# Recurrence chunk stages: the second heads' rounds run four rounds behind the first heads' rounds

## The reference

```python
def step(S, inp):
    w_t, k_t, v_t, a_t, b_t = inp[:5]
    sa = jnp.einsum('bhij,bhj->bhi', S, a_t)
    S = S * w_t[:, :, None, :] + sa[..., None] * b_t[:, :, None, :] + v_t[..., None] * k_t[:, :, None, :]
    y = jnp.einsum('bhij,bhj->bhi', S, inp[5]) if emit else None
    return S, y
...
S, ys = lax.scan(step, state0, xs, reverse=reverse)
```

## Time and profile before

| | us |
|---|---|
| median of 3 executions | 2481.49 (2477.02 to 2490.28) |
| the profiled execution: its time, its span | 2468.01, 2466.2 |
| `rc0`, 906.4 to 951.7 | 45.3 |
| `rc1`, 977.3 to 1023.5 | 46.2 |
| `rl0`, 1173.8 to 1224.7 | 50.9 |
| `rl1`, 1249.8 to 1301.1 | 51.3 |

### The profile page before, as it was taken

The page is one execution under the profiler, slowest core; times in us unless marked ns, Lnnn a source line. Parts: engine busy times, 40 slices in busy tenths (PEclk is TensorE's granted clock), DMA queues, the critical chain, the costliest instruction groups (busy, mean ns, idle before and its releaser), DMA issues. The chain is left out here.

```text
span 2466.2 us, 36848 instructions
## 1 busy us (share of the span) xinstructions
PE 1904.0 (77%) x15507; PEld 1233.3 (50%) x15507; DVE 864.4 (35%) x1268; ACT 637.2 (26%) x986; POOL 200.0 (8%) x279
## 2 busy tenths in 40 slices
PE   5999998668999877797888867667666666666665
PEld 5997996557888766696777752111111101101100
DVE  4654445765455565576564533000000000000000
ACT  3334444344324344333432310000000000000000
POOL 0100001010121043201550000000000000000000
PEclk9999999579999988798996968676766687677676
DMA  5654663016985410051002328999999999999996
GB/s 181 204 186 156 189 195 120 1 68 209 306 277 203 153 40 2 22 174 56 3 3 93 134 109 327 417 417 417 417 418 417 417 417 418 417 418 417 417 417 284
DMA packets 222497, 587.79 MB, mean 238 GB/s; under 512 B 11759, under 2 KB 144334, under 8 KB 189598
## 3 DMA queue, kind: packets, MB, share of 16 engines
q1 hardware_dynamic: 220518, 583.89, 62.8%
q10 hardware_dynamic: 1848, 2.01, 0.2%
HBM read 584.77 MB, written 1.09 MB: 238 GB/s over the span
## 5 line engine op out<-in xcount | busy, mean ns | idle before, releaser
L3056 PE MATMUL ps<-ex_ring,ex_xe 128*32 128x512 f32 x1536 | 282.5, 830 | 150.9 <-DMA ex_ring<-in_exp_w 150.9
L3131 DVE TENSOR_TENSOR ex_hid<-ps,ex_silu 128x512 f32<-128x512 f32 x16 | 11.1, 692 | 890.2 <-PE ps L3056 890.2
L3056 PEld LDWEIGHTS ps<-ex_ring,ex_xe 128*32 128x32 f32 x1536 | 36.7, 124 | 390.7 <-DMA ex_ring<-in_exp_w 368.3
L3077 PE MATMUL ps<-ex_ring,ex_ht 128*32 128x512 f32 x768 | 145.0, 853 | 86.1 <-DMA ex_ring<-in_exp_w 80.5
L209 PE MATMUL ps<-xt_hi,ffn_whi 128*128 128x256 f32 x704 | 205.1, 291 | 7.3 <-DVE xt_lo L372 7.3
L210 PE MATMUL ps<-xt_lo,ffn_whi 128*128 128x256 f32 x704 | 200.9, 285 | 0.0
L211 PE MATMUL ps<-xt_hi,ffn_wlo 128*128 128x256 f32 x704 | 200.6, 285 | 0.0
L181 DVE TENSOR_TENSOR ffn_wlo<-ring,ffn_whi 128x2048 fp32r<-128x2048 f32 x66 | 154.2, 2336 | 108.0 <-ACT ffn_whi L174 107.6
L174 ACT CAST ffn_whi<-ring 128x2048 fp32r<-128x2048 f32 x66 | 125.2, 1901 | 117.4 <-PE ps L211 102.8
L209 PEld LDWEIGHTS ps<-xt_hi,ffn_whi 128*128 128x128 f32 x704 | 136.4, 194 | 17.2 <-issue 17.0
L209 PE MATMUL ps<-mixin_whi,xt_hi 128*128 128x256 f32 (+1 forms) x496 | 137.7, 278 | 3.2 <-DVE xt_lo L372 3.2
(11 more groups left out here) (748 smaller groups left out, 3727.4 us busy)
## 6 DMA issues: line engine op xcount, KB each, us to landing
ex_ring<-in_exp_w SPq DMA_DIRECT2D x288, 1024.0 KB, 24.3
ring<-in_exp_w SPq DMA_DIRECT2D x96, 1024.0 KB, 24.8
ring<-in_w_in SPq DMA_DIRECT2D x55, 1024.0 KB, 5.2
ring<-in_ffn_w_gate SPq DMA_DIRECT2D x22, 1024.0 KB, 6.1
ring<-in_ffn_w_up SPq DMA_DIRECT2D x22, 1024.0 KB, 5.4
ring<-in_ffn_w_down SPq DMA_DIRECT2D x22, 1024.0 KB, 4.9
ffn_mod_tile<-in_mod_w SPq DMA_DIRECT2D x12, 1024.0 KB, 6.3
xn<-in_mod_w SPq DMA_DIRECT2D x12, 1024.0 KB, 6.8
```

The costliest lines, as they stand in the source:

```text
L3056: mm = mm_(ps[32 * q:32 * q + 32, 4 + u, :], xe[:, k], expert_slot(g, n)[:, 512 * q:512 * q + 512], start=k == 0, stop=k == KC - 1)
L3077: mm = mm_(ps[32 * q:32 * q + 32, 7, :], ht[:, k % 4, CAP * f:CAP * f + CAP], w[:, h, 512 * n:512 * n + 512], start=k == 0, stop=k == KC - 1)
L3131: v.tensor_tensor(hid[:], ps[:, 5, :], silu[:], ALU.mult).then_inc(S["hid"], 1)
```

## The change

```diff
-CHUNK_ROUNDS = 10
+CHUNK_ROUNDS, LAG = 10, 4
...
         def order():
-            for it in range(0, len(its), 2):
-                for r in range(CHUNK_ROUNDS):
-                    for j in range(2):
-                        yield its[it + j], r, it + j
+
+            n_steps = CHUNK_ROUNDS * len(its) // 2
+            for step in range(n_steps + LAG):
+                for j in range(2):
+                    k = step - LAG * j
+                    if 0 <= k < n_steps:
+                        it = 2 * (k // CHUNK_ROUNDS) + j
+                        yield its[it], k % CHUNK_ROUNDS, it
...
             if not ctx_only:
                 expand_g2(0)
+            expand(2)
+            if not ctx_only:
                 expand_g2(1)
-            expand(2)
             expand(3)
```

## The result

The changed kernel takes 2581.01 us (median of 4, 2578.94 to 2583.17) against 2485.89 for the kernel before: ratio 1.0385, 95% interval 1.0346 to 1.0424. That is some 95 us slower. The direction was forecast, the size wasn't: 2536 was forecast and 2556 was the upper end of the range.

What follows compares the result with a forecast made beforehand. The stages were taken as bound by each stream's chain of dependent rounds, with nothing beside them to hide growth. Stage growths of 14.9 + 14.5 + 13.7 + 12.8 = 55.9, taken as +55 on 2481.5, gave 2536 us, range 2516 to 2556.

Steps and rivals of the forecast that it cites:

- fronts: Rounds 0 to 3 of a stream's pass; four in a row, 11.6 us each in `rl` stages, replace two shared.
- the sum: Growth of the four chunk stages, 14.9 + 14.5 + 13.7 + 12.8 = 55.9 us, taken as +55.
- the wait for A's round 9: In an `rl` stage, A's second round 0 can't start until A's round 9 is done: 3.9 us.
- the wait for B's: In an `rl` stage, B's round 9 must finish before B's second round 0 starts: 2.1 us.
- The tail: End of an `rl` stage: A's round 9, B's rounds 5 to 9 alone, a wait on ACT; 12.5 us together.
- The costs set at nothing: POOL's new order and POOL's stage work, taken as hidden; possible `tm` diagonal wait 0 to 1 us per stage.
- POOL's order: POOL's swap of expand(2) and expand_g2(1) lets the lag of four run; claimed no gain, cost set at nothing.
- `tm` diagonals: POOL work behind `expand(1)`, ending near 25 us as A's first round 9 reaches DVE; 0 to 1 us per stage.
- the clock falls: Rival: PE's clock drops in the stages and behind them, 16 + 7 = 23 us more, 2559; chance 0.12.
- the neighbours: About four places outside the stages where 128x256 matmuls would slow at a lower clock, about 4 us each, 16 together.
- the forecast's own bounds: Range around the +55 us for stage pauses, ACT wait, front length and diagonals: +40 to +66, 2521 to 2548.
- PE is the bound and the stagger pays for itself: Rival: in the stages the other stream fills the fronts' waits; 49.6 against 50.9 us, -5 us in all, 2476; chance 0.03.

Runs made afterwards that it cites:

- entry fillers: Changed kernel with 3 unread extra matmuls behind each of A's rounds 0 to 3 of item 0, where A runs alone, 12 a stage; ratio 1.0263.
- the run with a lag of zero: Changed kernel with `LAG` 0: old order on PE, ACT and DVE, only POOL's expand(2) now ahead of expand_g2(1); ratio 1.0008.

## Why the prediction was right and wrong

**Right: the mechanism.** In-order engines, fronts taken apart, four in a row in place of two shared. With most of the clock back (0.88 to 0.95, entry fillers), the lag of four costs 252.6 - 193.7 = 58.9 us in the stages; the sum was 55.9. By stage, forecast and measured: `rc` 59, and 57.8 and 60.7; `rl` 65.8, and 66.7 and 67.4. The terms in `rl0` of the changed kernel, where it runs at 2.4 GHz: a front 11.6 and 11.7; the wait for A's round 9, 3.9 and 4.0; the wait for B's, 2.1 and 1.9. The tail, 12.5 and 13.6 (1297.88, B's round 4, to 1311.5), is at 0.50 from about 1306.5 on. The costs set at nothing were nothing: POOL's order by the run with a lag of zero, the DMA by the row of SP. The `tm` diagonals in `rl0` ended at 1270.07, just ahead of DVE's addition for A's round 9 at 1271.05, so they held nothing up, as narrowly as foreseen.

**Wrong: the price of the clock.** The step that failed is the clock's: the sum of +55 has it at nothing, and the rival "the clock falls", which should have caught that, was given 0.12 and +23 us. Two things in it were wrong.
- *Whether.* I argued from the earlier trace rows that rounds which run at 0.96 to 1.00 beside waits of up to 1.3 us can stand waits. But in those rows a second stream filled most of each wait. In the changed kernel A's front runs alone, with waits of 1 to 2 us in every round, and there the clock is lost (`rc1`, `rl0`, both at 1.00 for their first 4 to 6 us) or isn't regained (`rc0` and `rl1`, at 0.50 from the start). A row about two streams was read as one about one. And the means hid that the stages of before didn't hold the clock throughout either. `rc0` begins at 0.50 there too, but has A's and B's rounds 0 back to back and is at 1.00 from about 909.5 on; `rc1` loses the clock in its second front, behind a stretch in which PE waits more than it works. Busy time by window, kernel before, columns of the earlier trace rows:

```profile
906.40:909.00 2.60, 2.57 (x108) 2.60 (x112) 0.95 (x4) 0.00 (x0) 0.95 (x1) 0.50 0.03 6
1001.00:1005.00 4.00, 1.58 (x49) 1.19 (x43) 2.72 (x6) 2.70 (x9) 3.15 (x8) 1.00 0.01 4
1005.00:1009.00 4.00, 3.79 (x84) 3.14 (x80) 2.56 (x5) 1.85 (x6) 4.00 (x11) 0.57 0.00 0
```

  The Trainium skill, TensorE: Matmul & The Clock Gate, part 1, has the halved clock as the state that an idle PE falls back to. The falls in the lone fronts of `rc1` and `rl0` agree, and I had the rule in hand and set it aside; that `rc0` stays at 0.50 from 935 to 950, where PE has no idle time, idleness doesn't explain.
- *How much.* Inside the stages I priced only the tail of the `rl` ones, four 96-column rounds at most twice as long, 7 us, because there alone nothing hides PE; the context stages stood at nothing. I took the hidden rounds to stay hidden. At 1.2 GHz they don't: a step is A's round (1.90 us) plus B's (1.86) on one engine. Entry fillers alone give back 290.5 - 252.6 = 38 us in the stages of the profiled executions, 30 us by the ratios (1.0385 and 1.0263), and the clock isn't whole with them either. 30 of the 38 come from the context stages (78.2 to 57.8 and 70.3 to 60.7), and 8 from the `rl` stages; that 8 is near my 7 is chance, for the tails are at 0.50 with the fillers too. The other 16 us were meant for the neighbours, and these lost little: the time between the stages grew by 6.1 us and that behind the last by 2.7.

The forecast with this rival would have been 2559, still short. The case against the change was as strong as stated, though: even with most of the clock back, the ratio is 1.0234 to 1.0263. What keeps `rc0` at the lower level once PE has hardly a wait stays open.

Smaller slips, which move the forecast little: PE has 29% more time for its work by the sum (55.9 on 193.7), not 40%. The allowances named for the forecast's own bounds add up to +43 and +62, not +40 and +66. And the second pass of `rl0` looked 1.5 us longer than the first because its 26.2 us run to the stage's last evacuation and the 24.7 only to A's next round 0; counted alike, to the end of A's copy of `rm`, they are 25.2 and 24.5.

The rival in which PE is the bound and the stagger pays for itself fell as its chance said. The Trainium skill, Perfetto Trace Analysis, section Optimization Strategy, has it that interleaving regimes may help where the most-contended engine changes over time. It brought no gain here (lags of 1, 2 and 4: 1.0111, 1.0189, 1.0385): what bounds the stage of before is a chain of waits and not an engine, and both streams had been sharing those waits.

## What to carry to other kernels

Where two chains, each of dependent rounds, run side by side through the same engines in program order, the pairing to try first is the one in which like rounds share their latency; here a lag put one stream's short rounds behind the other's long ones, and cost its number of rounds at both ends besides. Before a change that makes PE wait more, price it at both clock levels: at the lower one, add up all of PE's work per step and see whether the chain or PE is longer, since what is hidden at 2.4 GHz may be the bound at 1.2. And a stage that must wait on short chains can be tested for a lost clock with a dozen useless matmuls in its waits.

## What the runs showed of the hardware

- **Added work made the kernel faster.** 12 matmuls per stage that nobody reads took the changed kernel from 1.0385 to 1.0263; 40 per stage took it to 1.0268. In the old order, whose clock is at 0.96 to 1.00 anyway, the same 40 cost 20 us.
- **The lower level can hold for a whole stage in which PE hardly waits.** `rc0` has matmuls in flight for 67.5 of 78.2 us and stays at 0.50, while the same work with fillers at the entry is at 0.91 with 45.5 of 57.8. So the share of time in which PE shows matmuls in flight doesn't tell which level it gets. In `rl0` and `rl1` the level did rise, once both streams ran. Timeline by window of `rl1` in the changed kernel, its first 30 us:

```profile
1338.70:1348.50 9.80, 5.97 (x124) 5.41 (x128) 3.28 (x7) 1.91 (x6) 4.59 (x11) 0.50 0.01 3
1348.50:1358.50 10.00, 7.71 (x160) 6.26 (x160) 2.23 (x5) 1.76 (x6) 0.70 (x2) 0.53 0.01 2
1358.60:1368.90 10.30, 8.05 (x157) 6.63 (x161) 6.09 (x13) 4.63 (x14) 8.53 (x16) 1.00 0.01 2
```

  By its busy time PE differs little between the second and the third window (0.77 and 0.78 of each), at 0.53 and 1.00. What makes the difference between the context and the latent stages wasn't tried further.
- **The lower level costs a latent round 0 more than a context one.** From A's first matmul to its round 1, in the changed kernel: context 4.08 us at 0.50 (`rc0`, 914.32 to 918.40) and 3.73 at 1.00 (`rc1`, 1019.36 to 1023.09); latent 6.78 at 0.50 (`rl1`, 1338.66 to 1345.44) and 4.97 at 1.00 (`rl0`, 1242.66 to 1247.63). That `rc0` has the same 4.08 in the kernel before says nothing, since it begins at 0.50 there too.
